# Tile 3's transpose ahead of tile 2's second one, tile 1's load behind tile 0's landing, and another order of the first squares and splits

## The chip, the cores and the metric

The kernel runs on one core of a Trainium2 chip. The metric is the device time of one execution in microseconds; before the change it was 253.89 us, the median of three runs (253.6 to 254.17). "SP" is the core's SyncE, which here does nothing but issue transfers.

## The reference, cut to what matters

One decoder layer over x (512 x 1024, float32). It normalises x by rows, projects it with w_in (1024 x 4096), runs four differential-attention heads and eight block-sparse heads on the result, gates both, projects with w_out and adds a normalised result to x:

```
h = rmsnorm(x, norm_pre_g)              # x * rsqrt(mean(x*x) + 1e-6) * g
u = h @ w_in                            # dq dk dv dg mq mk mv mg, 512 columns each
a = diff_attention(...) * silu(dg);  b = moba_attention(...) * silu(mg)
out = x + rmsnorm(concat(a, b) @ w_out, norm_post_g)
```

What is changed here touches only the start: rmsnorm of x, its transposed copy, and the first two groups of columns of w_in. No value that is computed changes.

## The kernel before, in words

The rows of x are four tiles of 128 (t = 0 to 3). Every float32 operand is split in two float16 halves, hi and lo, and TensorE forms hi*hi + hi*lo + lo*hi. `ht` holds the normalised x transposed, in its two halves. w_in comes in quarters: quarter n is a 512 KB load into stage buffer n % 4 (`load_quarter`), it covers two of the eight blocks of 128 rows of one group of 512 columns, and `split(n)` makes the halves of it: ScalarE w_hi (L749, L750), VectorE w_lo (L911, L913, or `split_row` L900 for one of the two rows). VectorE counts `split_lo`, and TensorE waits for its counts.

Work of TensorE is in units of 128 x 512 outputs. Unit 0 (tile 0) is multiplied in float32 straight from the stage buffers (`first_quarter`, L593). Ahead of its last quarter stand eight transposes of tile 1 (L540), which wait for `xs_ready`, VectorE's `x_norm(1)` (L978). Units 1, 2 and 3 (`late_lower_unit`, tiles 1, 2 and 3) have first 16 products with the upper half of the tile (L612), then 8 with the lower half (L619), so that the lower half may come late. Units from 4 on run L582.

The tiles get to `ht` by different ways. Tile 1: `x_norm(1)`, eight transposes on TensorE, `x_hi(1)` on ScalarE (L789), `x_lo(1)` on VectorE (L1013). Tiles 2 and 3: `xn_hi(t)` on ScalarE (L824) and `xn_lo(t)` on VectorE (L1019) write the normalised halves to `pt`, and SP issues a transposing DMA for each of them (`turn_x(t, h)`, L400; h = 0 is the upper half). TensorE waits for each of these four transfers by itself (L607, L617).

The scale of a tile is 1/rms of its rows. ScalarE squares the left half of x's columns (`x_square`, L736, which waits for the tile's load; it is an ACTIVATE and then a read of the accumulator), VectorE the right half (`x_half_square`, L964) and adds the two (`x_mean_square`, L972), GpSimd takes the power -1/2 (L482, `x_rstd`), and `x_norm`, `xn_hi` and `xn_lo` wait for it.

Each engine runs its instructions in the order in which they are written, and a wait holds all that stands behind it on that engine. So the order by hand on SP (L406 to L427), ScalarE (L836 to L859) and VectorE (L1113 to L1138) is what the change edits. SP's waits ahead of loads are there only to space them: they protect nothing.

Of the kernel before, what the change touches and what calls it, by code (L numbers as in the profile page):

```python
# [7 lines left out]
def bass_hymba_diff_moba_layer(  # L8
# [31 lines left out]
    TILES = SEQ // P  # L40
# [139 lines left out]
    with ctx:  # L180
# [3 lines left out]
        def sem(name):  # L184
            return ctx.enter_context(nc.semaphore(name))
# [78 lines left out]
        def x_columns(t):  # L264

            return score_ps[:, 2 * t:2 * t + 2, :].rearrange("p b (k s) -> p (b k) s", s=P)

        def x_half_rows(t):

            return x_halves[:, t - 2, :, :]  # L270

        x_loaded = [sem(f"x_loaded{t}") for t in range(TILES)]
# [9 lines left out]
        w_loaded = [sem(f"w_loaded{i}") for i in range(4)]  # L282
# [75 lines left out]
        def _(sp):  # L358
            def load_quarter(n):
                if n >= 4:  # L360
                    sp.wait_ge(split_lo, n - 3)
                if 4 <= n < 7:
                    sp.wait_ge(first_read, n - 3)
                elif n == 7:
                    sp.wait_ge(unit_done, 1)
                g, k = n // 4, 2 * (n % 4)
                if g < len(GROUPS):
                    col = GROUPS[g][2]
                    src = w_in_v[:, k:k + 2, col:col + WIDTH]
                else:  # L370
                    col = (g - len(GROUPS)) * WIDTH
                    src = w_out_v[:, k:k + 2, col:col + WIDTH]
                sp.dma_start(stage[:, n % 4, :].rearrange("p (k n) -> p k n", k=2), src)\
                    .then_inc(w_loaded[n % 4], 16)
# [23 lines left out]
            def turn_x(t, h):  # L398
                sp.wait_ge(xn_lo_ready if h else xn_hi_ready, t - 1)
                sp.dma_start_transpose(ht[:, h, :, t * P:(t + 1) * P], x_half_rows(t)[:, h, :])\  # L400
                    .then_inc(x_turned[t - 2][h], 16)

            def load_x(t):
                sp.dma_start(x_sb[:, t, :], x_v[t]).then_inc(x_loaded[t], 16)

            load_x(0)  # L406
            load_quarter(0)
            load_x(1)
            sp.wait_ge(x_loaded[0], 16)
            load_quarter(2)  # L410
            sp.wait_ge(w_loaded[0], 16)
            load_quarter(3)
            sp.wait_ge(w_loaded[1], 16)
            load_x(2)
            sp.wait_ge(x_loaded[1], 16)
            load_x(3)
            load_quarter(4)
            load_quarter(5)
            with nc.allow_non_contiguous_dma(reason="32 x 12 table, transposed once"):
                sp.dma_start(rel_t, rel_bias.rearrange("b h -> h b")).then_inc(rel_loaded, 16)  # L420
            for h in range(2):
                turn_x(2, h)
            turn_x(3, 0)
            load_quarter(6)
            turn_x(3, 1)
            load_quarter(7)
            load_quarter(8)  # L427
            sp.dma_start(lam_in[:, :, :], diff_lambda[0].partition_broadcast(P)).then_inc(lam_loaded, 16)
# [10 lines left out]
            for j in range(SLOTS):  # L439
# [3 lines left out]
                for n in SPLIT_IN_SLOT[j - 1] if j else []:  # L443
                    if n + 4 < QUARTERS:
                        load_quarter(n + 4)
                    else:
                        t = n + 4 - QUARTERS
# [280 lines left out]
        def _(act):  # L728
# [10 lines left out]
            def split(n):  # L739

                g, k = n // 4, 2 * (n % 4)
                act.wait_ge(w_loaded[n % 4], 16 * (n // 4 + 1))
                if g >= 3:
                    act.wait_ge(unit_done, LAST_OF_GROUP[g - 3] + 1)
                src = stage[:, n % 4, :].rearrange("p (k n) -> p k n", k=2)
                if g < len(GROUPS):
                    if n == 0:
                        act.wait_ge(g_scaled, 1)
                    nc.scalar.activation(w_hi[:, g % 3, k, :], src[:, 0, :], ACT.Copy, scale=g_cols[:, k:k + 1])  # L749
                    nc.scalar.activation(w_hi[:, g % 3, k + 1, :], src[:, 1, :], ACT.Copy,  # L750
                                         scale=g_cols[:, k + 1:k + 2]).then_inc(split_hi, 1)
                else:
                    nc.scalar.activation(w_hi[:, g % 3, k:k + 2, :], src, ACT.Copy,
                                         scale=W_SCALE).then_inc(split_hi, 1)
# [27 lines left out]
            def x_hi(t):  # L782
                if t == 1:
                    act.wait_ge(xt_ready, 1)
                    src = x_columns(1)
                else:
                    act.wait_ge(x_scaled_ready, 1)
                    src = x_scaled
                nc.scalar.activation(ht[:, 0, :, t * P:(t + 1) * P], src, ACT.Copy).then_inc(ht_hi_ready, 1)  # L789
# [32 lines left out]
            def xn_hi(t):  # L822
                act.wait_ge(x_rstd_ready, t + 1)
                nc.scalar.activation(x_half_rows(t)[:, 0, :], x_sb[:, t, :], ACT.Copy,  # L824
                                     scale=x_rstd[:, t:t + 1]).then_inc(xn_hi_ready, 1)

            def x_square(t):
                act.wait_ge(x_loaded[t], 16)

                square(x_sq[:, t:t + 1], x_sb[:, t, 0:DM // 2], x_squared, t + 1)  # L830
# [4 lines left out]
                                w_in_v[:, 2:4, first:first + WIDTH]).then_inc(w_loaded[1], 16)  # L835
            x_square(0)  # L836
            split(0)
            x_square(1)
            split(1)
            split(2)  # L840
            split(3)
            x_square(2)
            x_hi(1)
            x_square(3)
            xn_hi(2)
            unit(0)
            xn_hi(3)
            for u in range(1, FIRST_UNITS):
# [45 lines left out]
        def _(dve):  # L894
            def split_row(n, part):

                g, k = n // 4, 2 * (n % 4) + part
                dve.wait_ge(split_hi, n + 1)
                src = stage[:, n % 4, part * WIDTH:(part + 1) * WIDTH]
                ins = nc.vector.scalar_tensor_tensor(w_lo[:, g % 3, k, :], src, g_cols[:, k:k + 1],  # L900
                                                     w_hi[:, g % 3, k, :], ALU.mult, ALU.subtract)
                if part == 1:
                    ins.then_inc(split_lo, 1)

            def split(n):

                g, k = n // 4, 2 * (n % 4)
                dve.wait_ge(split_hi, n + 1)
                src = stage[:, n % 4, :].rearrange("p (k n) -> p k n", k=2)
                if g < len(GROUPS):  # L910
                    nc.vector.scalar_tensor_tensor(w_lo[:, g % 3, k, :], src[:, 0, :], g_cols[:, k:k + 1],  # L911
                                                   w_hi[:, g % 3, k, :], ALU.mult, ALU.subtract)
                    nc.vector.scalar_tensor_tensor(w_lo[:, g % 3, k + 1, :], src[:, 1, :],  # L913
                                                   g_cols[:, k + 1:k + 2], w_hi[:, g % 3, k + 1, :], ALU.mult,
                                                   ALU.subtract).then_inc(split_lo, 1)
                else:
                    nc.vector.scalar_tensor_tensor(w_lo[:, g % 3, k:k + 2, :], src, W_SCALE,
                                                   w_hi[:, g % 3, k:k + 2, :], ALU.mult,
                                                   ALU.subtract).then_inc(split_lo, 1)
# [48 lines left out]
            def x_mean_square(t):  # L968

                dve.wait_ge(x_squared, t + 1)  # L970
                dve.wait_ge(x_half_squared, t + 1)
                nc.vector.tensor_tensor(x_ms[:, t:t + 1], x_sq[:, t:t + 1], x_half_sq[:, t:t + 1],  # L972
                                        ALU.add).then_inc(x_mean, 1)

            def x_norm(t):

                dve.wait_ge(x_rstd_ready, t + 1)
                nc.vector.tensor_scalar(x_sb[:, t, :], x_sb[:, t, :], x_rstd[:, t:t + 1], 1.0,  # L978
                                        ALU.mult, ALU.mult).then_inc(xs_ready, 1)
# [26 lines left out]
            def x_lo(t):  # L1006
                dve.wait_ge(ht_hi_ready, HT_COUNT[t])
                cols = slice(t * P, (t + 1) * P)
                src = x_columns(1)
                if t == 0:  # L1010
                    dve.wait_ge(x_scaled_ready, 1)
                    src = x_scaled
                nc.vector.tensor_tensor(ht[:, 1, :, cols], src, ht[:, 0, :, cols],  # L1013
                                        ALU.subtract).then_inc(ht_ready, 1)
# [108 lines left out]
            split(0)  # L1123
            x_half_square(1)
            x_mean_square(1)
            x_norm(1)
            split(1)
            split_row(2, 0)
            x_half_square(2)
            x_mean_square(2)  # L1130
            split_row(2, 1)
            x_half_square(3)
            x_mean_square(3)
            split(3)
            x_lo(1)
            unit(0)
            xn_lo(2)
            xn_lo(3)  # L1138
# [88 lines left out]
```

## Time and profile before

| What | Before |
|---|---|
| Median of three runs | 253.89 us |
| The profiled execution, its own time | 253.66 us |
| Its span, first to last instruction | 251.9 us |
| TensorE busy | 245.6 us (98%) |
| VectorE busy | 177.9 us (71%) |
| ScalarE busy | 142.9 us (57%) |
| GpSimd busy | 32.3 us (13%) |

The span leaves out 1.76 us of the execution's own time. TensorE's busy time is by modelled ends of pipelined matmuls; a start of one matmul and the start of the next tell how dense they stand. In a timeline "x8" merges eight instructions in a row, "<-" in brackets names what ended the idle time before an instruction, and an engine with a q behind its name (SPq) is its sequencer, with the DMAs that it issues.

### The profile page before, as it was taken

What the parts mean: (1) busy time and instruction counts of PE and PEld (TensorE: products, weight loads), DVE (VectorE), ACT (ScalarE), POOL (GpSimd) and SP (SyncE); (2) the same over time, 40 slices, a digit from 0 to 9 for tenths busy, and PEclk for the clock granted to TensorE, in tenths of its full rate; (3) what the DMA queues carried; (4) which work ended last, traced back from release to release, by engine and by line L of the source; (5) the groups of instructions that cost most, each with busy time, mean ns of one, the idle gap of its engine ahead of it and who ended that gap; (6) DMA issues with size and microseconds to landing.
All of it is one profiled execution on the core that took longest, in us unless ns stands there. A gap on an engine that the chain in (4) does not pass through costs nothing.

```text
span 251.9 us, 4449 instructions
## 1 busy us (share of the span) xinstructions
PE 245.6 (98%) x1564; PEld 123.6 (49%) x1564; DVE 177.9 (71%) x396; ACT 142.9 (57%) x336; POOL 32.3 (13%) x73
## 2 busy tenths in 40 slices
PE   8999999999999999999999999999999999999991
PEld 8544444445444554544455444454444444555570
DVE  2899685687477788868777767978787896835313
ACT  3895485274456666574676595577566665611110
POOL 1259100000000420040041033000000000111101
PEclk9999999999999999999999999999999999999997
DMA  7976989705565545453935553569849786982422
GB/s 265 392 212 128 306 292 359 239 17 135 107 174 149 181 115 140 111 190 106 200 104 139 144 158 116 140 187 182 176 103 200 196 182 158 199 208 42 125 86 83
DMA packets 59674, 42.47 MB, mean 169 GB/s; under 512 B 45808, under 2 KB 46072, under 8 KB 59652
## 3 DMA queue, kind: packets, MB, share of 16 engines
q1 hardware_dynamic: 59364, 41.66, 62.3%
q10 hardware_dynamic: 288, 0.53, 0.6%
q8 instruction: 13, 0.21, 0.3%
q14 instruction: 9, 0.07, 0.1%
HBM read 29.04 MB, written 2.13 MB: 124 GB/s over the span
## 4 chain that ended last, share of the span: by engine, by line
PE 97%; issue 1%; DVE 0%; DVEq 0%; ACT 0%; POOLq 0%; POOL 0%
PE unit_ps L582 72%; PE score_ps L638 6%; PE o_ps L659 5%; PE unit_ps L612 4%; PE unit_ps L593 3%; PE unit_ps L619 2%; PE unit_ps L547 2%; PE unit_ps L713 1%; PE score_ps L540 1%; PE score_ps L713 1%; DVE area L1108 0%; DVEq L180 0%; ACT junk L736 0%; POOLq L180 0%; PE unit_ps L666 0%
## 5 line engine op out<-in xcount | busy, mean ns | idle before, releaser
L582 PE MATMUL unit_ps<-area,w_hi 128*128 128x512 f16 x256 | 76.2, 379 | 0.0
L797 ACT ACTIVATE arena<-arena,negmax 128x512 f32<-128x512 f32 (+3 forms) x64 | 35.4, 554 | 49.8 <-DVE negmax L1035 49.7
L582 PE MATMUL unit_ps<-w_hi,area 128*128 128x512 f16 x192 | 60.3, 379 | 0.0
L582 PE MATMUL unit_ps<-area,w_lo 128*128 128x512 f16 x128 | 48.5, 379 | 0.0
L582 PEld LDWEIGHTS unit_ps<-area,w_hi 128*128 128x128 f16 x256 | 24.1, 98 | 27.2 <-issue 1.1
L582 PE MATMUL unit_ps<-w_lo,area 128*128 128x512 f16 x96 | 36.4, 379 | 0.0
L1035 DVE CUSTOM_DVE_ANT_0 arena<-score_ps,strips 128x512 f32<-128x512 f32 (+3 forms) x64 | 28.6, 484 | 9.4 <-PE score_ps L638 9.4
L911 DVE SCALAR_TENSOR_TENSOR w_lo<-stage,g_cols,w_hi 128x512 f16<-128x512 f32 x31 | 23.4, 754 | 10.8 <-ACT w_hi L750 10.6
L582 PEld LDWEIGHTS unit_ps<-w_hi,area 128*128 128x128 f16 x192 | 18.8, 98 | 21.9 <-issue 1.2
L749 ACT ACTIVATE w_hi<-stage,g_cols 128x512 f16<-128x512 f32 x32 | 22.7, 710 | 5.4 <-DMA stage<-in_w_in_dram 5.4
L913 DVE SCALAR_TENSOR_TENSOR w_lo<-stage,g_cols,w_hi 128x512 f16<-128x512 f32 x31 | 24.1, 778 | 0.0
L750 ACT ACTIVATE w_hi<-stage,g_cols 128x512 f16<-128x512 f32 x32 | 22.6, 707 | 0.0
L1064 DVE TENSOR_TENSOR arena<-arena 128x512 f16<-128x512 f32 (+5 forms) x32 | 21.0, 655 | 1.5 <-ACT arena L811 1.5
L811 ACT ACTIVATE arena<-arena 128x512 f16<-128x512 f32 (+5 forms) x32 | 18.9, 592 | 3.6 <-DVE arena L1055 3.5
L582 PEld LDWEIGHTS unit_ps<-area,w_lo 128*128 128x128 f16 x128 | 12.5, 98 | 15.1
L582 PE MATMUL unit_ps<-w_hi,q_hi 128*128 128x512 f16 x64 | 19.9, 379 | 0.0
L659 PE MATMUL o_ps<-v_hi,pt 128*128 128x64 f16 (+1 forms) x240 | 18.9, 202 | 0.0
L659 PEld LDWEIGHTS o_ps<-v_hi,pt 128*128 128x128 f16 x240 | 15.5, 98 | 3.8
L736 ACT ACTIVATE junk<-unit_ps 128x512 f16<-128x512 f32 (+1 forms) x8 | 4.5, 564 | 22.6 <-PE unit_ps L582 22.0
L659 PE MATMUL o_ps<-v_lo,pt 128*128 128x64 f16 (+1 forms) x120 | 16.2, 202 | 0.0
L504 POOL TENSOR_SCALAR sub_ms<-sub_sq 128x4 f32<-128x4 f32 x4 | 0.8, 193 | 110.6 <-ACT junk L736 110.6
L582 PE MATMUL unit_ps<-w_hi,q_lo 128*128 128x512 f16 x48 | 14.9, 379 | 0.0
(114 smaller groups left out, 360.4 us busy)
## 6 DMA issues: line engine op xcount, KB each, us to landing
stage<-in_w_in_dram SPq DMA_DIRECT2D x31, 512.0 KB, 4.0
stage<-in_w_out_dram SPq DMA_DIRECT2D x8, 512.0 KB, 4.2
arena<-in_x_dram SPq DMA_DIRECT2D x4, 512.0 KB, 5.1
strips<-bias_rows SPq DMA_DIRECT2D x4, 512.0 KB, 4.2
stage<-in_x_dram SPq DMA_DIRECT2D x4, 512.0 KB, 4.4
out_dram<-area SPq DMA_DIRECT2D x3, 512.0 KB, 2.7
strips<-bias_rows SPq DMA_DIRECT2D x1, 1024.0 KB, 7.3
stage<-in_w_in_dram ACTq DMA_DIRECT2D x1, 512.0 KB, 6.9
```

The costliest lines, as they stand in the source:

```text
L582: last = nc.tensor.matmul(bank, a, b, start=(k == 0 and n == 0), stop=(k == KT - 1 and n == 2))
L612: nc.tensor.matmul(bank, ht[:, 0, k, rows], b[:, g % 3, k, :], start=(k == 0 and b is w_hi), stop=False)
L638: last = nc.tensor.matmul(score_ps[:, bank, col:col + n], a[part, ch, rows], b[part, ch, 0:n], start=first, stop=final)
L659: last = nc.tensor.matmul(o_ps[:, o % 2, col:col + width], a, b[:, k, src], start=(k == 0 and n == 0), stop=(k == t and n == 2))
L749: nc.scalar.activation(w_hi[:, g % 3, k, :], src[:, 0, :], ACT.Copy, scale=g_cols[:, k:k + 1])
L750: nc.scalar.activation(w_hi[:, g % 3, k + 1, :], src[:, 1, :], ACT.Copy, scale=g_cols[:, k + 1:k + 2]).then_inc(split_hi, 1)
L797: nc.scalar.activation(probs[:, i % 2, m, 0:n], probs[:, i % 2, m, 0:n], ACT.Exp, bias=negmax[:, i, m:m + 1], scale=-1.0, accum_out=sums[: ...
L811: nc.scalar.activation(hi, probs[:, i % 2, 0:1 + r, 0:n], ACT.Copy).then_inc(p_hi_ready, 1)
L911: nc.vector.scalar_tensor_tensor(w_lo[:, g % 3, k, :], src[:, 0, :], g_cols[:, k:k + 1], w_hi[:, g % 3, k, :], ALU.mult, ALU.subtract)
L913: nc.vector.scalar_tensor_tensor(w_lo[:, g % 3, k + 1, :], src[:, 1, :], g_cols[:, k + 1:k + 2], w_hi[:, g % 3, k + 1, :], ALU.mult, ALU.s ...
L1035: nc.vector.tensor_tensor_reduce(out=probs[:, i % 2, m, 0:n], in0=score_ps[:, bank, col:col + n], in1=strips[:, h, 0:n][:, ::-1], scale=-1 ...
L1064: nc.vector.tensor_tensor(lo, probs[:, i % 2, 0:1 + r, 0:n], hi, ALU.subtract)\
```

## The change

SP issues tile 1's load only when tile 0 has landed, and each quarter's load one landing later than before (quarter 2 at the landing of quarter 0, quarter 3 at that of quarter 1, x's tiles 2 and 3 at that of tile 1). The four transposing DMAs go out as (2, hi), (3, hi), (2, lo), (3, lo), all ahead of quarter 6's load; before they went (2, hi), (2, lo), (3, hi), quarter 6, (3, lo). ScalarE does `split(1)` ahead of `x_square(1)`, `x_hi(1)` ahead of `x_square(2)`, and `xn_hi(2)` ahead of `x_square(3)`. VectorE does the first row of quarter 1's split ahead of `x_norm(1)` and the second behind it, quarter 2's split whole ahead of tile 2's square, and quarter 3's split and `x_lo(1)` ahead of tile 3's.

```diff
             load_x(0)
             load_quarter(0)
+            sp.wait_ge(x_loaded[0], 16)
             load_x(1)
-            sp.wait_ge(x_loaded[0], 16)
+            sp.wait_ge(w_loaded[0], 16)
             load_quarter(2)
-            sp.wait_ge(w_loaded[0], 16)
+            sp.wait_ge(w_loaded[1], 16)
             load_quarter(3)
-            sp.wait_ge(w_loaded[1], 16)
+            sp.wait_ge(x_loaded[1], 16)
             load_x(2)
-            sp.wait_ge(x_loaded[1], 16)
             load_x(3)
             load_quarter(4)
             load_quarter(5)
...
             for h in range(2):
-                turn_x(2, h)
-            turn_x(3, 0)
+                for t in range(2, TILES):
+                    turn_x(t, h)
             load_quarter(6)
-            turn_x(3, 1)
             load_quarter(7)
...
             x_square(0)
             split(0)
+            split(1)
             x_square(1)
-            split(1)
             split(2)
             split(3)
+            x_hi(1)
             x_square(2)
-            x_hi(1)
+            xn_hi(2)
             x_square(3)
-            xn_hi(2)
             unit(0)
             xn_hi(3)
...
             x_half_square(1)
             x_mean_square(1)
+            split_row(1, 0)
             x_norm(1)
-            split(1)
-            split_row(2, 0)
+            split_row(1, 1)
+            split(2)
             x_half_square(2)
             x_mean_square(2)
-            split_row(2, 1)
+            split(3)
+            x_lo(1)
             x_half_square(3)
             x_mean_square(3)
-            split(3)
-            x_lo(1)
             unit(0)
```

## Rows read from the trace of the kernel before

**Rows 1.** The page: the chain of work that ended last, by engine.
```profile
PE 97%; issue 1%; DVE 0%; DVEq 0%; ACT 0%; POOLq 0%; POOL 0%
```

**Rows 2.** TensorE's timeline; columns: start us, us, engine, line, operation, tiles, idle before.
```profile
11.98 1.04 PE L540 MATMUL score_ps<-ident,arena 128*128 128x128 f32 x8
...
17.92 0.38 PE L612 MATMUL unit_ps<-w_lo,area 128*128 128x512 f16 x1
...
23.50 1.89 PE L619 MATMUL unit_ps<-w_hi,area 128*128 128x512 f16 x8
```

**Rows 3.** TensorE's weight loads, same columns; who released them stands in brackets.
```profile
18.31 0.76 PEld L619 LDWEIGHTS unit_ps<-w_hi,area 128*128 128x128 f16 x5 [0.50 <-DVE area L1013]
...
23.37 0.67 PEld L619 LDWEIGHTS unit_ps<-w_hi,area 128*128 128x128 f16 x4 [0.20 <-DMA area<-pt]
```

**Rows 4.** SP's issues in its timeline; then L400's four times from issue to landing.
```profile
4.09 2.29 SPq L373 DMA_DIRECT2D stage<-in_w_in_dram  x2
...
16.54 1.34 SPq L400 DMA_TRANSPOSE area<-pt  x1
...
20.14 1.23 SPq L400 DMA_TRANSPOSE area<-pt  x1
...
21.41 1.34 SPq L400 DMA_TRANSPOSE area<-pt  x1
...
DMA to landing us min/median/max: 3.1/3.2/4.5
```

**Rows 5.** ACT's issue of w_in's second quarter, its landing, and x's four landings.
```profile
1.35 0.41 ACTq L834 DMA_DIRECT2D stage<-in_w_in_dram  x1
...
DMA to landing us min/median/max: 6.9/6.9/6.9
...
DMA to landing us min/median/max: 3.3/5.1/6.4
```

**Rows 6.** ScalarE's timeline.
```profile
8.71 0.71 ACT L749 ACTIVATE w_hi<-stage,g_cols 128x512 f16<-128x512 f32 x1
...
12.90 0.63 ACT L736 ACTIVATE junk<-arena 128x512 f16<-128x512 f32 x1 [0.42 <-DMA arena<-in_x_dram]
...
13.44 0.19 ACT L736 ACTIVATION_READ_ACCUMULATOR junk<-arena 128x1 f32 x1
...
13.53 1.00 ACT L789 ACTIVATE area<-score_ps 128x1024 f16<-128x1024 f32 x1
...
15.36 1.15 ACT L824 ACTIVATE pt<-arena,x_rstd 128x1024 f16<-128x1024 f32 x1 [0.21 <-POOL x_rstd L482]
...
16.42 0.67 ACT L772 ACTIVATE v_hi<-unit_ps,first_scale 128x512 f16<-128x512 f32 x1
```

**Rows 7.** VectorE's timeline.
```profile
9.02 0.68 DVE L964 CUSTOM_DVE_ANT_0 heads_out<-arena 128x512 f32<-128x512 f32 x1
...
9.81 0.16 DVE L972 TENSOR_TENSOR x_ms<-x_sq,x_half_sq 128x1 f32<-128x1 f32 x1
...
10.65 0.75 DVE L978 TENSOR_SCALAR arena<-arena,x_rstd 128x1024 f32<-128x1024 f32 x1 [0.67 <-POOL x_rstd L482]
...
14.18 0.74 DVE L900 SCALAR_TENSOR_TENSOR w_lo<-stage,g_cols,w_hi 128x512 f16<-128x512 f32 x1
...
15.71 0.75 DVE L911 SCALAR_TENSOR_TENSOR w_lo<-stage,g_cols,w_hi 128x512 f16<-128x512 f32 x1
...
17.04 1.22 DVE L1013 TENSOR_TENSOR area<-score_ps,area 128x1024 f16<-128x1024 f32 x1
```

**Rows 8.** GpSimd's timeline.
```profile
6.90 0.56 POOL L482 TENSOR_TENSOR x_rstd<-x_ms,minus_half 128x1 f32<-128x1 f32 x1 [5.43 <-DVE x_ms L972]
...
10.06 0.55 POOL L482 TENSOR_TENSOR x_rstd<-x_ms,minus_half 128x1 f32<-128x1 f32 x1 [2.24 <-DVE x_ms L972]
...
14.34 0.99 POOL L482 TENSOR_TENSOR x_rstd<-x_ms,minus_half 128x1 f32<-128x1 f32 x1 [3.73 <-DVE x_ms L972]
```

**Rows 9.** Stretches: busy time by engine, granted TensorE clock, DMA share, GB/s.
```profile
246.00:252.00 6.00, 0.40 (x4) 0.11 (x2) 1.97 (x5) 0.48 (x2) 0.55 (x1) 0.71 0.23 87
```

## The prediction, made before the changed kernel ran

> **What bounds the kernel now.** First the page's chain of waits: 97% of it is TensorE [rows 1]. Then TensorE's timeline over the first 30 us, where the change lies: from 6.73 us on the matmuls stand at their own pace (0.43 us a float32 record, 0.215 us a float16 product), with one hole of 0.17 us: the record at 17.92 gives way at 18.14, and the next stands at 18.31, behind the lower half of tile 1 (x_lo(1)) [rows 2, 3]. So an edit at the start can win 0.17 us at most, and whatever makes TensorE wait there is paid in full at the end, for nothing behind has slack to give back. The waits of the weight loads show how near that is: the lower half of tile 2 arrived by DMA 0.13 us before its first matmul, and the weight load stood waiting for it for 0.20 us [rows 2, 3]. SP's timeline says why: that transposing DMA was issued at 20.14 and landed 3.2 us later, 23.34 [rows 4]. It is the tightest thing in the stretch, and the change puts another transfer ahead of it.
>
> **How SP serves transposes.** One transposing DMA holds SP's queue: 20.14 to 21.41 is 1.27 us from one to the next, and the third, issued at once behind the second, still landed 3.2 us after its own issue [rows 4]. After the change (3, hi) stands ahead of (2, lo). SP therefore waits for xn_hi(3), issues it, and issues (2, lo) 1.27 us later. That costs nothing if xn_hi(3) is done by 20.14 - 1.27 = 18.87 us. Before, it stood behind the record at 16.42 (0.67), takes 1.15 itself, and so was done by 18.15 [rows 6]. The question is when it ends now.
>
> **The chain to xn_hi(3), step by step** (all in us from the span's start).
> 1. ScalarE has split(1) ahead of x_square(1). Quarter 1's load is issued on ScalarE's own queue at 1.35 and landed at 8.25 [rows 5]. I keep 8.25: the other queue still holds x's tile 0 and quarter 0, and tile 1's load, now issued at tile 0's landing (4.07), comes before these are through. Split: two activations of 0.71 that overlap their neighbour by 0.09, so 1.23; square: 0.54 and 0.19 for the accumulator [rows 6]. So split at 8.28, square at 9.51, done 10.24; before, 8.81.
> 2. VectorE's mean at 10.28 instead of 9.81; GpSimd starts 0.25 after that (9.81 to 10.06) [rows 7, 8], at 10.53.
> 3. The power took 0.55 us beside an idle VectorE, 0.56 beside an operation that reads PSUM and one SBUF operand, and 0.99 beside L900, which reads two operands from SBUF [rows 7, 8]. Now split_row(1, 0), the same L900, stands exactly there: 0.99, end 11.52. The GPSIMD Engine Reference (Specifications) of the Trainium skill says that the SBUF interfaces are shared with VectorE, with contention for instructions that have two SBUF inputs; the trace agrees (0.99 against 0.55), and the sum with its rule is the same 0.44 worse than with a free GpSimd.
> 4. x_norm(1) at 11.56, 0.75 long [rows 7], end 12.31; TensorE's transposes 0.05 later at 12.36, where they began at 11.98 [rows 2]: TensorE loses 0.38.
> 5. Transposes 1.04 to 13.40 [rows 2]; x_hi(1) 13.44, 0.91 to the next (1.00 less the 0.09 by which ScalarE's records overlap) [rows 6]. Being ahead of x_square(2) now, it holds the square, which ran at 12.90 before, to 14.35; done 15.08.
> 6. Mean 15.12, power 15.37 to 16.36 (split(3) beside it reads two SBUF operands: 0.99), xn_hi(2) 16.39 [rows 6, 8]; it was 15.36. It ends 1.15 later, and its DMA lands near 20.7 instead of 19.65. That is a wait of its own, which the next one covers.
> 7. xn_hi(2) now stands ahead of x_square(3): 16.39 + 1.06 = 17.45, done 18.18. Before it was done at 15.15: this is the largest move of all. VectorE's half comes behind split(3) and x_lo(1): 15.20 + 1.33 + 1.13 = 17.66, mean 0.79 later [rows 7], 18.45. That is the later of the two.
> 8. Power 18.70 to 19.26 (0.56: beside it stands unit(0)'s lower half, which reads PSUM and one SBUF operand), xn_hi(3) 19.29 to 20.44, (3, hi) issued 20.47, (2, lo) 21.74, landed 24.94, matmul 0.16 later, 25.10.
> Before it was 23.50 [rows 2]. **Sum: +1.60 us.** The 0.38 of step 4 is inside it, and so is the 0.17 that x_lo(1), now ready by 17.7, gives back.
>
> **The other edits.** Quarter 2 is issued at quarter 0's landing, 6.0 (now quarter 3's time, the end of the pair of issues less the 0.38 of one) instead of 4.09; TensorE needs it four float32 records before 11.98, at 10.27 [rows 2, 4]. Its place in the queue is the same, behind tile 1, and tile 1 lands as before, so I take its landing as unchanged: nothing. Bounds: 3.3 us after issue at best, no gain; 6.9 at worst (12.9), 2.6 us lost [rows 4, 5]. Quarter 3 is issued at 8.3 instead of 6.0 and is wanted at 13: at best nothing, at worst (15.2) 2.2. Tile 2's load goes from 8.26 to about 8.7: with the median 5.1 it lands at 13.8, ahead of its square at 14.35; with 6.4 [rows 5] at 15.1, +0.75. Behind SP's new waits stand only the later loads, whose readers come later still. (3, lo) now goes 1.27 behind (2, lo), lands near 26.2, and is wanted at 30: nothing. Quarter 6 is issued about 24.3 instead of 22.85, quarter 7 about 24.9 instead of 24.76, with TensorE itself 1.6 later: nothing. VectorE's waits for the means hold unit(0) and xn_lo(2) near 18.5, about where they were (18.17, 18.83).
>
> **Rivals.**
> - *Quarter 1 lands earlier,* because tile 1 isn't in its way (7.8 or sooner). Then mean(1) is at 9.81, x_norm ends 11.84, transposes start at 11.98 as before, and everything is 0.38 earlier: +1.2. For it: it took 6.9 us, the longest of the loads at the start, while x's tile 0 took 3.3 [rows 5]. Against: tile 1's load joins again before quarter 0 is through. Even with the powers at 0.55 it stays near 1.2, for VectorE's half of tile 3 then ends last (18.07).
> - *A load late by its later issue* (quarter 2, or tile 2), or the last power 0.99 beside xn_lo(2): +0.4 to +1.2 on top, 255.7 to 256.7.
> - *Not slower: the transfers have room.* If (3, hi) is issued by 18.87 us, (2, lo) goes out at 20.14 as before and all that is left is the hole closed: 253.7. This needs xn_hi(3) 1.6 us sooner than my chain, that is, tile 3's square not behind xn_hi(2), or a SP that doesn't stand for 1.27 us. ScalarE's order excludes the first, rows 4 the second. What speaks for it is that a chain of eight steps, read from one execution, can be off in its handoffs; that makes tenths, not 1.6.
> - *The clock.* TensorE would now stand 0.4 and then about 1.2 us in two or three places. The only long idle stretch shown is the end: 0.40 us of work in 6.0, granted 0.71 on the mean [rows 9], so between its 2.4 and 1.2 GHz levels. All other stretches are at 1.00, none with a hole of 1 us in it. If the clock fell to 1.2 GHz for half a unit's 24 products (12 of 0.215), these would take twice as long: +2.6 more, 258. The page TensorE: Matmul & The Clock Gate (HAM oscillation) of the Trainium skill names holes in the work as what throttles the engine, longer ones than I expect here; no row shows a hole of this size.
>
> **How the numbers follow.** Forecast (+1.6): 0.50. Quarter 1 early (+1.2): 0.20. Late load or power (+2.0 to 2.8): 0.15. Not slower: 0.12, of which 0.09 within 0.2% and 0.03 for a gain over that, for which no row has room. Clock: 0.03. The profiled execution is 253.66, so its twin is 253.66 + 1.60 = 255.26; the median is 0.23 above it: 253.89 + 1.60 = 255.5. The range goes from the early quarter 1 with 0.3 for what I round (254.7) to 256.5, one moderate late load. A measurement of this kernel tells 0.2% (0.5 us) from no change. The likely cases are all above that: slower 0.88, same 0.09, faster 0.03.
>
> **What would show it.** In the changed profile: ScalarE's x_square(1) behind L750 and near 9.5 (near 8.5 if quarter 1 is early); L482's second record 0.99; transposes L540 of tile 1 at 12.3 (11.98 if early); xn_hi(3) starting near 19.3; SP's L400 issues near 17.6, 20.5, 21.7 and 23; a wait of TensorE's L619 for the DMA area<-pt of about a microsecond; then L582 as dense as before. I am wrong if the third issue of L400 is at 20.2 or earlier, or if L619 of unit 2 starts by 23.6.

## The result, and the profile after

The changed kernel took 255.65 us (median of six runs, 255.06 to 256.34) beside 253.96 us for the kernel before in the same rounds: ratio 1.0057, 95% interval 1.0037 to 1.0076, so 1.45 us slower (0.57% of 253.96; the medians differ by 1.69). The forecast was 255.5, +1.60. The profiled execution took 255.14 us, 1.48 more than the one of before (253.66); its span is 253.3 us.

Lines of the changed kernel behind L425 have a number one lower (L1013 is L1012 there). The page's chain by engine, the answer to [rows 1]:

```profile
PE 87%; DMA 6%; ACT 2%; DVE 2%; issue 1%; POOL 0%; DVEq 0%; ACTq 0%; POOLq 0%
```

TensorE no longer fills the chain: 6% are DMAs, 4% work of the other engines. That is not time in which TensorE stood. From 24.98 us on the chain is TensorE's as before; what changed is the 25 us ahead of it, where the chain now leads from a wait of TensorE back through the transfer and the engines that fed it. TensorE's timeline shows how long it waits, the answer to [rows 2]:

```profile
10.25 1.96 PE L592 MATMUL unit_ps<-stage,gates 128*128 128x512 f32 x4 [0.30 <-DMA stage<-in_w_in_dram]
12.05 1.04 PE L539 MATMUL score_ps<-ident,arena 128*128 128x128 f32 x8
...
18.20 1.89 PE L618 MATMUL unit_ps<-w_hi,area 128*128 128x512 f16 x8
20.71 0.38 PE L611 MATMUL unit_ps<-w_hi,area 128*128 128x512 f16 x1 [0.62 <-issue]
...
24.98 1.90 PE L618 MATMUL unit_ps<-w_hi,area 128*128 128x512 f16 x8 [0.65 <-DMA area<-pt]
```

The transposes of tile 1 stand at 12.05 (11.98 before), unit 1's lower half at 18.20 (18.31), unit 2 at 20.71 (20.05) and its lower half at 24.98 (23.50). The loss of 1.48 us is there in full at 24.98. It arises in two waits: by the starts, 0.66 us are lost up to unit 2, and 0.82 more between its two halves (the 0.62 and 0.65 in the brackets are counted from modelled ends, so they are smaller). The row at 20.71 names no releaser; that it waited for (2, hi) is read from that transfer's landing, 3.2 us after its issue at 17.47. The hole of 0.30 for quarter 2 is no part of the loss: the float32 products had begun 0.45 us sooner than before (6.28 instead of 6.73). Behind 24.98 nothing is lost or won: the last matmul starts at 247.61 instead of 246.13, again 1.48 later.

The waits of the weight loads, then SP's four transposing DMAs in a row, and the third of them ((2, lo)) with its landing, answers to [rows 3, 4]:

```profile
PEld unit_ps L618 <- DMA area<-pt: 1.1, 1, 1.1
```
```profile
17.47 6.88 SPq L400 DMA_TRANSPOSE area<-pt  x4
```
```profile
L400 SPq DMA_TRANSPOSE area<-pt x1: 1335/1335/1335, 21.6 to 21.6; - x1
DMA to landing us min/median/max: 3.3/3.3/3.3
```

(2, lo) is issued at 21.6 instead of 20.14 and lands 3.3 us later. ScalarE, VectorE and GpSimd, the answers to [rows 6 to 8]:

```profile
8.63 0.61 ACT L735 ACTIVATE junk<-arena 128x512 f16<-128x512 f32 x1
...
14.29 0.62 ACT L735 ACTIVATE junk<-arena 128x512 f16<-128x512 f32 x1
...
16.29 1.15 ACT L823 ACTIVATE pt<-arena,x_rstd 128x1024 f16<-128x1024 f32 x1 [1.29 <-POOL x_rstd L481]
...
19.18 1.15 ACT L823 ACTIVATE pt<-arena,x_rstd 128x1024 f16<-128x1024 f32 x1 [0.56 <-POOL x_rstd L481]
```
```profile
9.74 0.74 DVE L899 SCALAR_TENSOR_TENSOR w_lo<-stage,g_cols,w_hi 128x512 f16<-128x512 f32 x1
10.93 0.75 DVE L977 TENSOR_SCALAR arena<-arena,x_rstd 128x1024 f32<-128x1024 f32 x1 [0.45 <-POOL x_rstd L481]
...
13.93 0.69 DVE L963 CUSTOM_DVE_ANT_0 heads_out<-arena 128x512 f32<-128x512 f32 x1 [0.26 <-DMA arena<-in_x_dram]
...
18.36 0.16 DVE L971 TENSOR_TENSOR x_ms<-x_sq,x_half_sq 128x1 f32<-128x1 f32 x1
...
19.33 2.47 DVE L1018 SCALAR_TENSOR_TENSOR pt<-arena,x_rstd,pt 128x1024 f16<-128x1024 f32 x2
```
```profile
9.91 0.99 POOL L481 TENSOR_TENSOR x_rstd<-x_ms,minus_half 128x1 f32<-128x1 f32 x1 [2.89 <-DVE x_ms L971]
...
18.60 0.55 POOL L481 TENSOR_TENSOR x_rstd<-x_ms,minus_half 128x1 f32<-128x1 f32 x1 [2.34 <-DVE x_ms L971]
```

x_square(1) starts at 8.63, not at 9.51 as forecast: quarter 1 had landed at 7.06. The power for tile 1 takes 0.99 us beside L899. xn_hi(3) starts at 19.18 (forecast 19.29).

One reading needs care. The chain of waits of this execution gives the time up to 21.64 to VectorE:

```profile
19.41 2.22 DVE pt L1018 x2
21.64 3.29 DMA area<-pt
```

(Columns: start us, us, what.) SP's wait ahead of (2, lo) is for xn_lo(2), the first of these two instructions, and that was done near 20.6. What held SP to 21.64 was its own issue of (3, hi) from 20.36. An inferred releaser is the last event of the awaited kind; when it ended long before, look at what stood ahead on the queue. The first experiment settles it.

### The profile page after: what moved, and what is told of

Read it like the earlier page. It is cut to its first block, busy times and chain, and to the rows that moved or that the text cites. A ratio compares the mean times of both kernels' runs of the same rounds, so it can differ in the third digit from the quotient of the medians.

```text
span 253.3 us, 4449 instructions
## 1 busy us (share of the span) xinstructions
PE 245.0 (97%) x1564; PEld 122.1 (48%) x1564; DVE 178.4 (70%) x396; ACT 143.1 (56%) x336; POOL 32.1 (13%) x73
## 4 chain that ended last, share of the span: by engine, by line
PE 87%; DMA 6%; ACT 2%; DVE 2%; issue 1%; POOL 0%; DVEq 0%; ACTq 0%; POOLq 0%
PE unit_ps L581 72%; PE score_ps L637 6%; PE o_ps L658 5%; DMA stage<-in_w_in_dram 4%; PE unit_ps L618 1%; PE unit_ps L611 1%; DMA area<-pt 1%; PE unit_ps L712 1%; DVE pt L1018 1%; ACT junk L735 1%; PE score_ps L712 1%; ACT area L788 0%; POOL x_rstd L481 0%; DVE area L1107 0%; DVE v_lo L954 0%
```

## The experiments

Theory 1 is the prediction's: (2, lo) waits on SP behind (3, hi), because the new order of ScalarE and VectorE makes xn_hi(3) late. Rivals: either of the two orders costs by itself, or the late loads do. The change has three parts, and seven of the eight combinations ran beside the kernel before (the ratio of the first line is the result above; before was 253.76 to 253.96 in all rounds).

| loads | engines | SP's transposes | ratio to before | 95% interval |
|---|---|---|---|---|
| new | new | new | 1.0057 | 1.0037 to 1.0076 |
| new | new | old | 1.0027 | 1.0008 to 1.0046 |
| old | old | new | 0.9998 | 0.9984 to 1.0012 |
| old | new | old | 1.0029 | 1.0014 to 1.0044 |
| new | old | old | 1.0033 | 1.0019 to 1.0048 |
| old | new | new | 1.0068 | 1.0044 to 1.0091 |
| new | old | new | 1.0025 | 1.0008 to 1.0043 |

**SP's order taken back.** The diff against the changed kernel:

```diff
             for h in range(2):
-                for t in range(2, TILES):
-                    turn_x(t, h)
+                turn_x(2, h)
+            turn_x(3, 0)
             load_quarter(6)
+            turn_x(3, 1)
```

> The changed kernel with SP's order of transposing DMAs as before: (2,hi), (2,lo), (3,hi), quarter 6, (3,lo). Theory 1, (2,lo) waits behind (3,hi) on SP: (2,lo) is then issued at xn_lo(2)'s end, near 20.6 us instead of 21.6, lands near 23.8, and what is left is only the late (2,hi): unit 2 starts at 20.7 as in the changed kernel and its lower half runs without a hole at 24.2 (24.98 there, 23.50 before). So 0.7 to 0.8 us faster than the changed kernel, 0.7 slower than before. Rival, the squares' and splits' order is the whole cause: within 0.3 us of the changed kernel.

254.38 us, ratio 1.0027. TensorE's timeline, unit 2's two halves:

```profile
20.77 0.38 PE L612 MATMUL unit_ps<-w_hi,area 128*128 128x512 f16 x1 [0.91 <-issue]
...
24.22 1.89 PE L619 MATMUL unit_ps<-w_hi,area 128*128 128x512 f16 x8
```

No hole ahead of the lower half, which stands 0.76 us sooner. SP issued (2, lo) at 20.7. The difference of the ratios, 0.0030, is 0.76 us. The two intervals overlap, but nine of the twelve runs of this kernel are below the shortest of the changed one (255.06). As theory 1 has it; the DVE entry in the chain was not the holder.

**SP's order alone.**

```diff
             for h in range(2):
-                turn_x(2, h)
-            turn_x(3, 0)
+                for t in range(2, TILES):
+                    turn_x(t, h)
             load_quarter(6)
-            turn_x(3, 1)
```

> The kernel before with the new order of transposing DMAs alone. Theory 1: the order costs only if xn_hi(3) is done after 18.87 us. In the kernel before it is done near 18.1, so (3,hi) goes out near 18.2, (2,lo) still at 20.1, unit 2's lower half still at 23.5: within 0.2 us of before. Rival, a second transposing DMA in flight slows (2,lo) or SP's standing on it costs by itself: 0.5 to 1.3 us slower than before.

253.81 us, ratio 0.9998. (3, hi) went out at 18.2 and (2, lo) at 20.2, 3.2 us to landing: a second transposing DMA in flight did not slow it here. The order costs only behind a late xn_hi(3).

**ScalarE's and VectorE's order alone** (the change's two last hunks on the kernel before).

> The kernel before with ScalarE's and VectorE's new order alone (SP as before, loads and transposes). Theory 1: quarter 1 lands at 8.25 us again, so x_square(1) is late: the transposes of tile 1 start near 12.35 instead of 11.98; xn_hi(2) starts near 16.4, (2,hi) lands near 20.8, unit 2 starts 20.9 and its lower half 24.3: 0.7 to 0.8 us slower than before. Rival, the order of the engines is harmless without the new order on SP: within 0.2 us of before. Rival, it is the whole cause: 1.5 us slower.

254.59 us, ratio 1.0029: 0.74 us, theory 1.

```profile
12.47 1.09 PE L540 MATMUL score_ps<-ident,arena 128*128 128x128 f32 x8 [0.28 <-DVE arena L978]
...
20.93 0.38 PE L612 MATMUL unit_ps<-w_hi,area 128*128 128x512 f16 x1 [0.37 <-issue]
24.39 1.89 PE L619 MATMUL unit_ps<-w_hi,area 128*128 128x512 f16 x8
```

Here the steps 1 to 4 of the prediction stand as they were written: with x's tile 1 loaded at once quarter 1 came at 8.4, x_norm(1) was late, and the transposes waited for it (12.47; forecast 12.36).

**The loads alone** (the first hunk on the kernel before).

> The kernel before with the new waits ahead of the loads alone. Theory 1: nothing to 0.3 us slower; quarter 1 lands before 7.4 us instead of 8.25, quarter 2 near 10.1 instead of 9.6 and TensorE waits 0.3 us for it, from a start of the float32 products that is earlier or later by quarter 0's landing. Rival, the late loads carry half of the loss: 0.6 us slower or more.

254.74 us, ratio 1.0033: 0.84 us, more than I had given it. The rival was right.

```profile
15.42 0.39 PE L612 MATMUL unit_ps<-w_hi,area 128*128 128x512 f16 x1 [0.71 <-ACT area L789]
```
```profile
13.73 0.63 ACT L736 ACTIVATE junk<-arena 128x512 f16<-128x512 f32 x1 [0.86 <-DMA arena<-in_x_dram]
```
```profile
13.73 0.69 DVE L964 CUSTOM_DVE_ANT_0 heads_out<-arena 128x512 f32<-128x512 f32 x1 [0.48 <-DMA arena<-in_x_dram]
```

Tile 2 landed at 13.7 instead of 12.87, its square stood ahead of x_hi(1), and unit 1 began at 15.42 instead of 14.69; but VectorE stood idle for tile 2 as well. What came late was not tile 2's issue, which was 0.2 us sooner than before (8.05 instead of 8.26). Quarters 2 and 3 were issued at 5.88 and 6.8 instead of 4.09 and 6.0, and were still under way with it; that they are the reason was not tried by itself. A later run takes the two waits for tile 2 apart.

**The changed kernel with the old loads** (its first hunk taken back).

> The changed kernel with the loads as before: ScalarE's, VectorE's and SP's transposes in the new order. Theory 1: this is the chain of the prediction with quarter 1 at 8.25: x_norm(1) done near 12.3, xn_hi(3) from 19.3 to 20.5, (3,hi) 20.5, (2,lo) 21.8, landed 25.0, unit 2's lower half at 25.1 to 25.3: 1.5 to 1.8 us slower than before, as the changed kernel, which shows that the new loads neither help nor hurt once the order of the engines is new. Rival, the loads carry a part of the changed kernel's loss: 0.8 to 1.0 us slower only.

255.40 us, ratio 1.0068, 1.7 us. Theory 1 again, now with every number of the prediction's chain:

```profile
12.40 1.09 PE L539 MATMUL score_ps<-ident,arena 128*128 128x128 f32 x8 [0.27 <-DVE arena L977]
...
25.13 1.90 PE L618 MATMUL unit_ps<-w_hi,area 128*128 128x512 f16 x8 [0.66 <-DMA area<-pt]
```
```profile
17.63 6.89 SPq L400 DMA_TRANSPOSE area<-pt  x4
```

The forecast was 12.36 and 25.10. The loads change nothing that can be told once the other parts are new (1.0068 and 1.0057, intervals overlapping), though alone they cost 0.84 us. The traces say why the costs don't add: held-back loads bring quarter 1 sooner, which frees the new order of ScalarE (transposes at 12.05 instead of 12.40), and the new order of VectorE has splits to do while tile 2 is on its way (0.26 us idle in the changed kernel, 0.48 with the loads alone). SP's order is what costs in both: of the twelve runs of the two engines' order alone, eleven are below the shortest run of this kernel (255.23).

**The changed kernel with the old order of ScalarE and VectorE** (last two hunks taken back).

> The changed kernel with ScalarE's and VectorE's order as before: the loads and SP's transposes in the new order. Theory 1: with tile 3's square ahead, xn_hi(3) is done near 18.6 and (3,hi) out before (2,lo) is ready, so SP's order costs nothing and the time is that of the loads alone: 0.7 to 1.0 us slower than before. Rival, SP's order costs with any late tile 2: 1.5 us slower or more.

254.71 us, ratio 1.0025, like the loads alone (1.0033). Theory 1 holds: (3, hi) was out at 19.1, and its issue was over before xn_lo(2) was done near 20.9.

**ScalarE's square of tile 3 ahead again**, on the changed kernel:

```diff
             x_square(2)
-            xn_hi(2)
             x_square(3)
+            xn_hi(2)
```

> The changed kernel with ScalarE's x_square(3) ahead of xn_hi(2) again; VectorE and SP as changed. Theory 1: VectorE's own half of tile 3, behind split(3) and x_lo(1), ends last (mean at 18.36 in the changed kernel, ScalarE's square done at 18.06), so ScalarE's order alone buys nothing: within 0.2 us of the changed kernel. Rival, ScalarE's order holds tile 3: xn_hi(3) starts 2 us sooner and 0.8 us are won.

255.00 us, ratio 1.0049 (1.0024 to 1.0073). VectorE's mean and ScalarE's xn_hi(3):

```profile
17.93 0.16 DVE L971 TENSOR_TENSOR x_ms<-x_sq,x_half_sq 128x1 f32<-128x1 f32 x1
```
```profile
18.76 1.15 ACT L823 ACTIVATE pt<-arena,x_rstd 128x1024 f16<-128x1024 f32 x1 [1.17 <-POOL x_rstd L481]
```

VectorE's half still ended last and xn_hi(3) still waited 1.17 us for the power. The intervals overlap; the 0.4 us by which this execution is ahead are there from its start on (quarter 0 landed at 5.79 instead of 6.16, and mean(1) stood at 9.29 instead of 9.66).

**Tile 3's square ahead on both engines.** To the edit above this adds, on VectorE:

```diff
             x_mean_square(2)
+            x_half_square(3)
+            x_mean_square(3)
             split(3)
             x_lo(1)
-            x_half_square(3)
-            x_mean_square(3)
```

> The changed kernel with tile 3's square ahead on both engines: x_square(3) ahead of xn_hi(2) on ScalarE, x_half_square(3) and x_mean_square(3) ahead of split(3) on VectorE; loads and SP's new order of transposing DMAs stay. Theory 1: the mean of tile 3 is there near 15.9 us, xn_hi(3) follows unit(0) near 18 instead of 19.2 and (3,hi) goes out near 19.2, (2,lo) near 20.5 instead of 21.6; unit 2 starts at 20.7 as in the changed kernel and its lower half runs on at 24.2: 0.7 us faster than the changed kernel, although SP's order is the changed one. Rival, SP's order costs by itself: no gain. x_lo(1) comes 0.9 us later than in the changed kernel and may cost 0.2 us.

254.81 us, ratio 1.0033 (1.0017 to 1.0048): 0.6 us of the 1.45 come back, about as expected, though the intervals overlap (nine of its twelve runs are below 255.06). The trace is not the one that I expected.

```profile
18.21 0.39 PE L611 MATMUL unit_ps<-w_hi,area 128*128 128x512 f16 x1 [0.77 <-DVE w_lo L912]
...
19.34 1.90 PE L618 MATMUL unit_ps<-w_hi,area 128*128 128x512 f16 x8
21.08 0.38 PE L611 MATMUL unit_ps<-w_hi,area 128*128 128x512 f16 x1
...
24.53 1.89 PE L618 MATMUL unit_ps<-w_hi,area 128*128 128x512 f16 x8
```
```profile
14.54 0.69 DVE L963 CUSTOM_DVE_ANT_0 heads_out<-arena 128x512 f32<-128x512 f32 x1 [0.72 <-DMA arena<-in_x_dram]
...
15.86 0.69 DVE L963 CUSTOM_DVE_ANT_0 heads_out<-arena 128x512 f32<-128x512 f32 x1 [0.35 <-DMA arena<-in_x_dram]
...
18.07 1.22 DVE L1012 TENSOR_TENSOR area<-score_ps,area 128x1024 f16<-128x1024 f32 x1
```

(3, hi) went out at 19.3 and (2, lo) at 21.2, so the hole ahead of unit 2's lower half is gone. In its place VectorE waited 0.72 us for tile 2 and 0.35 for tile 3, and all that stood behind came late. TensorE lost 0.93 us (by the starts, 17.06 to 18.21) to the second row of quarter 3's split, did four products, and lost 0.26 more to x_lo(1), which began at 18.07. The late loads, hidden behind the split in the changed kernel, come out when the squares go first.

**GpSimd's power without VectorE beside it**, on the changed kernel:

```diff
-            split_row(1, 0)
             x_norm(1)
-            split_row(1, 1)
+            split(1)
```

> The changed kernel with VectorE idle during GpSimd's power for tile 1: x_norm(1) ahead of both rows of split(1). Theory 1, the 0.99 us of the power come from VectorE's two-operand work beside it: the second record of L482 is 0.55, x_norm(1) starts 0.4 us sooner; TensorE's transposes do not (they stood behind quarter 2's landing), so the time is within 0.2 us of the changed kernel. Rival, the power's length is chance or is set by something else: 0.99 again. Rival, x_norm(1) was on the path: 0.4 us faster.

255.36 us, ratio 1.0062 (1.0039 to 1.0084).

```profile
9.51 0.56 POOL L481 TENSOR_TENSOR x_rstd<-x_ms,minus_half 128x1 f32<-128x1 f32 x1 [2.40 <-DVE x_ms L971]
```

This is GpSimd's timeline. The power is 0.56 with VectorE idle and 0.99 in the changed kernel beside L899: it is VectorE's work beside it, not chance. The time did not move. The profiled execution was among the long ones, and shows something else:

```profile
25.81 1.90 PE L618 MATMUL unit_ps<-w_hi,area 128*128 128x512 f16 x8 [1.50 <-DMA area<-pt]
```
```profile
L400 SPq DMA_TRANSPOSE area<-pt x1: 2153/2153/2153, 21.6 to 21.6; - x1
DMA to landing us min/median/max: 4.1/4.1/4.1
```

(2, lo), issued at 21.6 as in the changed kernel, landed 4.1 us later instead of 3.3, after (3, hi) had taken 4.5, and TensorE waited 1.50 us.

**Which half of the late loads costs.** The loads alone, and in ScalarE's order:

```diff
-            x_square(2)
             x_hi(1)
+            x_square(2)
```

> The new waits ahead of the loads (as in the run of the loads alone) and one edit of ScalarE's order: x_hi(1) ahead of x_square(2). Theory 1: the loads alone cost because tile 2 landed at 13.7 us and its square stood ahead of x_hi(1), so that unit 1 began at 15.4 instead of 14.7; with x_hi(1) ahead this start comes back to 14.6 or so. Tile 2's own chain stays late (mean near 14.6), (2,hi) lands near 20.3 and unit 2's lower half stands at 23.9 to 24.0: 0.2 us better than the loads alone, 0.5 worse than before. Rival, the start of unit 1 was the whole cost: within 0.2 us of before.

254.89 us, ratio 1.0033 (1.0016 to 1.0050): exactly that of the loads alone.

```profile
14.23 0.38 PE L612 MATMUL unit_ps<-w_hi,area 128*128 128x512 f16 x1
...
18.92 1.90 PE L619 MATMUL unit_ps<-w_hi,area 128*128 128x512 f16 x8
...
24.11 1.89 PE L619 MATMUL unit_ps<-w_hi,area 128*128 128x512 f16 x8
...
30.38 1.90 PE L619 MATMUL unit_ps<-w_hi,area 128*128 128x512 f16 x8 [0.93 <-DMA area<-pt]
```

Unit 1's start came back and bought nothing: behind VectorE's idle time for tile 2 (0.86 us) quarter 3's split came late, for which TensorE lost 0.95 us up to 17.78, and then x_lo(1), for which it lost 0.26 up to 18.92, and unit 2's lower half stood at 24.11 (24.06 in the loads alone). The loads cost through VectorE. This execution lost another 0.93 us at 30.38: (3, lo), in the old order behind quarter 6's load, landed 6.3 us after its issue, and in the other runs with SP's old order after 4.5 to 4.7. That is the one thing that SP's new order avoids: in the seven runs with it (3, lo) landed within 3.3 us.

**Only tile 1's load held back.** On the kernel before, with `split(1)` ahead of `x_square(1)` and `x_hi(1)` ahead of `x_square(2)` on ScalarE:

```diff
             load_quarter(0)
-            load_x(1)
             sp.wait_ge(x_loaded[0], 16)
+            load_x(1)
```

> A version from the findings: of the loads only tile 1's is held back to tile 0's landing (quarters 2 and 3 and x's tiles 2 and 3 as before), ScalarE does split(1) ahead of x_square(1) and x_hi(1) ahead of x_square(2), x_square(3) stays ahead of xn_hi(2); VectorE's order and SP's transposing DMAs are those of before. Theory 1: quarter 1 lands before 7.4 us, quarter 2 by 9.7 and tile 2 by 12.9, so nothing waits that did not before: within 0.2 us of before, at best 0.2 faster. Rival, any delay of tile 1's load pushes all later ones back by its length: 0.3 to 0.8 us slower, as with all four waits moved.

254.63 us, ratio 1.0031 (1.0009 to 1.0053), runs from 253.73 to 256.56. Neither theory: the profiled execution was as fast as before, most others were not, and which of their transfers came late was not seen. What it does show is what an early TensorE is worth:

```profile
14.12 0.38 PE L612 MATMUL unit_ps<-w_hi,area 128*128 128x512 f16 x1
...
18.37 1.90 PE L619 MATMUL unit_ps<-w_hi,area 128*128 128x512 f16 x8
```
```profile
17.10 1.22 DVE L1013 TENSOR_TENSOR area<-score_ps,area 128x1024 f16<-128x1024 f32 x1
```

Unit 1 began 0.57 us sooner than before, and its lower half 0.06 later, because VectorE reached x_lo(1) at 17.10 (17.04 before).

**Filling VectorE's hole.** VectorE is what holds TensorE up to unit 2, so on the kernel before, its wait for the first power gets one row of a split:

```diff
+            split_row(1, 0)
             x_norm(1)
-            split(1)
+            split_row(1, 1)
             split_row(2, 0)
```

> A version from the findings: the kernel before with the first row of quarter 1's split in the hole of 0.67 us that VectorE has ahead of x_norm(1), and nothing else. Theory 1: the power of tile 1 goes from 0.55 to 0.99, x_norm(1) is 0.4 later, which TensorE does not see (its transposes come 0.6 later), and all of VectorE behind it is 0.2 sooner: (2,lo) out near 19.9 instead of 20.14, the hole of 0.17 before unit 1's lower half closed: 0.1 to 0.2 us faster than before, at the edge of what can be told. Rival, x_norm(1) comes on the path in the executions in which TensorE starts early: 0.2 us slower.

253.72 us beside 253.79, ratio 0.9987 (0.9970 to 1.0004).

```profile
18.16 1.89 PE L619 MATMUL unit_ps<-w_hi,area 128*128 128x512 f16 x8
...
23.34 1.89 PE L619 MATMUL unit_ps<-w_hi,area 128*128 128x512 f16 x8
```

No hole ahead of 18.16, and the lower half of unit 2 0.16 us ahead of before. The size is the expected one, but the interval takes in no change: not shown to be faster. Nor did it come about as written:

```profile
10.18 0.75 DVE L900 SCALAR_TENSOR_TENSOR w_lo<-stage,g_cols,w_hi 128x512 f16<-128x512 f32 x1 [0.49 <-ACT w_hi L750]
```

The row's other half was ready on ScalarE only at 10.14. So VectorE stood for 0.49 us all the same, GpSimd's power had begun before the row (9.77) and took 0.55, not 0.99, and x_norm(1) was 0.2 later. Behind it VectorE was 0.47 ahead (x_lo(1) at 16.57), more than the 0.2 expected, and TensorE, now dense, could use no more than its hole of 0.17.

## Why the prediction was right, point by point

**The bound.** Right: TensorE had no slack behind, and the loss at 24.98 is the loss at the end (1.48 us in both). Of the changed kernel's six runs three took 255.06 to 255.38 us and three 255.92 to 256.34. The trace is of one of the shorter; what lengthened the others was not seen (a candidate stands in the last section).

**SP's queue.** Right in mechanism and price. (3, hi) at 20.36, (2, lo) at 21.64, landing 24.93; forecast 20.47, 21.74, 24.94. The rule behind the 18.87 us is that xn_hi(3) must be done one issue (1.27) ahead of xn_lo(2), and it is borne out from both sides. Done at 18.2 the order is free (SP's order alone). Done at 19.1 and 19.2 it is free too, because there xn_lo(2) itself was done only at 20.9 and 21.1 (the old order of the engines, and tile 3's square ahead on both). Done at 20.3 to 20.5, with xn_lo(2) at 20.6 to 20.7, it costs 0.76 us (new loads) to 1.0 (old loads, 1.0068 against 1.0029).

**Steps 1 and 4.** Wrong: quarter 1 landed at 7.06, not 8.25.

```profile
1.35 5.71 DMA stage<-in_w_in_dram
```

(From the chain of waits: start us, us, what.) The rival "quarter 1 lands earlier" was the right one, and by its +1.2 the time would have been 255.1. I argued that tile 1's load would join again before quarter 0 was through; with x's first load and quarter 0 alone in the other queue for 2.7 us more (tile 1 was issued at 4.38, not 1.65), the load from ScalarE's queue gained 1.2 us.

**The other edits.** It says "nothing" for quarter 2, which landed at 10.1. TensorE waited 0.30 us for it, but had begun 0.45 sooner, so the transposes stood only 0.07 later than before. Wrong is the "nothing" for quarter 3: it landed at 12.1, ScalarE's split waited 0.67 us for it, and x_hi(1), behind that split, began at 13.39 although the transposes were over at 13.09. This put ScalarE's chain back to nearly where my wrong quarter 1 had it: transposes 12.05 instead of 12.36, but x_square(2) at 14.29 against 14.35. Two errors of 0.3 to 0.4 us cancelled. That the total is closer than its parts is luck. Tile 2 was issued at 8.36, only 0.1 later than before, and landed near 13.9 (forecast 13.8, but from a later issue and a shorter flight). For the loads alone the text would have said 0 and they cost 0.84; that tile 2 is covered holds for ScalarE's order, as written, and not for VectorE, which was idle for it.

**Step 3.** Right: 0.99 beside L899, 0.56 with VectorE idle.

**Steps 5 and 6.** Right within 0.1: xn_hi(2) 16.29 (16.39), landing of (2, hi) 20.65 (20.7). "The next one covers" it was half the truth: 0.7 us of the loss is this wait, and remains when the other is removed.

**Steps 7 and 8.** VectorE was the later of the two, as said, and ScalarE's order alone gives nothing. The remark that ScalarE's move was the largest was beside the point. The means at 18.36 (18.45), the power 0.55.

**The other rivals.** The clock did not fall: it is 1.00, TensorE's 2.4 GHz level, from 20 to 30 us, which has both waits in it.

```profile
20.00:30.00 10.00, 8.73 (x41) 3.80 (x41) 8.74 (x12) 6.25 (x10) 7.78 (x31) 1.00 0.85 214
```

## What to carry to other kernels

A transfer that occupies the issuing queue is free only if its data is ready a whole issue before the next one's; work out that time and compare it with the chain that makes the data, not with when it was ready before another part of the same change moved it. When several delays lie on one chain their costs need not add (0.74 and 0.84 us alone, 0.68 together), so one part taken back says little about another. And if an engine is 98% busy, ask which other engine feeds it in the stretch: here VectorE's standing for tile 2, a load that TensorE did not yet need, came out at the end in three kernels (the loads alone, the same with x_hi(1) ahead, and tile 3's square ahead on both). It did not where ScalarE's half of the square ended later anyway: with the power free VectorE stood 0.43 us for tile 2, and the time did not move.

## What the runs showed of the hardware

- A transposing DMA held SP for 1.23 to 1.34 us and landed 3.0 to 3.3 us after the start of its issue in most cases, but 4.5 to 4.7 and once 6.3 right behind quarter 6's load. Three profiles have a longer issue: 2.15 us with the power free, where that transfer landed after 4.1 us and the one ahead of it after 4.5; 2.19 (landed after 3.5) with the old order of the engines; and 2.05 (landed after 3.4) in the last experiment, where the transfer ahead had already landed. So it isn't tied to several of them close together, and its cause is open. It can carry some of the spread of the changed kernel (255.06 to 256.34), but that was not tried.
- ScalarE's queue issued quarter 1 near 1.35 us in every kernel. It landed after 5.4 to 5.8 us in all nine profiles in which SP held tile 1's load back to tile 0's landing, and after 6.9 to 7.3 in all five in which it did not.
- GpSimd's power took 0.99 us beside a VectorE instruction that reads two operands from SBUF, and 0.55 or 0.56 otherwise. In the rows of 0.99 it had begun 0.16 or 0.17 us behind that instruction and ended 0.41 to 0.42 us behind its end; in the last experiment it began first, L900 came 0.14 us before its end, and it took 0.55. That fits a GpSimd that waits until VectorE's instruction is through, rather than one that runs slower beside it, but no run here varies the start to tell the two apart.
- With the same waits and the same work, the first eight transposes of tile 0 took 1.73 us before and 1.03 with only tile 1's load held back, both at a granted clock of 1.00. Over all profiles unit 0's first product stood anywhere from 5.94 to 6.73. In those two executions the difference does not reach the end: VectorE's mean of tile 1 was 0.52 us sooner in the second (9.29 instead of 9.81), its mean of tile 2 no longer (14.16 and 14.10).
